# One program per engine for each mixer: attention heads between the last projections, the scan behind the heads

## What is computed

```python
def _mixer(x, w_in, ..., w_out, band_bias, valid):
    u = x @ w_in
    ...
    u_conv, u_lru, q, k, v = jnp.split(u, [o1, o2, o3, o4], axis=-1)
    y_conv = _conv_module(u_conv, ...)
    y_lru = _recurrent(u_lru, ...)
    y_attn = _swa(q, k, v, band_bias, valid, sinks)
    return jnp.concatenate([y_conv, y_lru, y_attn], axis=-1) @ w_out
```

## Time and profile before

| | us |
|---|---|
| three runs | 2514.08, 2515.64, 2520.54 (median 2515.64) |
| profiled execution | 2516.15 |
| its span, first to last instruction | 2514.3 |
| TensorE busy in the span | 2396.6 (95%), 14866 matmuls |
| VectorE busy | 1877.7 (75%) |
| ScalarE busy | 1245.8 (50%) |
| GpSimd busy | 60.3 (2%) |

### The profile page before, as it was taken

How to read it: one execution, slowest core, us unless ns; L and a number is a source line. 1 busy time by engine, 2 the same in 40 slices (tenths; PEclk the granted TensorE clock), 3 DMA queues, 4 the chain that set the end, 5 groups by cost and what they waited for, 6 DMA issues and landing times. The chain is left out here.

```text
span 2514.3 us, 39398 instructions
## 1 busy us (share of the span) xinstructions
PE 2396.6 (95%) x14866; PEld 2130.2 (85%) x14866; DVE 1877.7 (75%) x2802; ACT 1245.8 (50%) x2014; POOL 60.3 (2%) x91
## 2 busy tenths in 40 slices
PE   7998969999989999998999999999999988999998
PEld 3877847888889999886799998899998967999997
DVE  4887578999977776588677776577875796777765
ACT  5345437887734554246345554245552355445541
POOL 0011011000000000000000000000000000000000
PEclk8999979999999999999999999999999999999999
DMA  6774559999943333230223234314334312233332
GB/s 233 278 252 151 197 223 357 412 411 412 347 126 93 104 107 126 87 110 34 68 85 118 85 118 145 87 54 119 91 91 153 93 62 68 68 93 101 110 121 81
DMA packets 312858, 381.50 MB, mean 152 GB/s; under 512 B 16845, under 2 KB 229485, under 8 KB 312567
## 3 DMA queue, kind: packets, MB, share of 16 engines
q1 hardware_dynamic: 303192, 344.59, 40.6%
q0 software_dynamic: 6896, 26.22, 2.8%
q10 hardware_dynamic: 2606, 8.47, 0.8%
HBM read 345.65 MB, written 33.57 MB: 151 GB/s over the span
## 5 line engine op out<-in xcount | busy, mean ns | idle before, releaser
L1740 PE MATMUL PS<-xT_hi,w_part_hi 128*128 128x256 f32 (+1 forms) x1472 | 436.9, 297 | 9.3 <-DVE w_part_lo L1736 3.6
L1742 PE MATMUL PS<-xT_hi,w_part_lo 128*128 128x256 f32 (+1 forms) x1472 | 431.8, 293 | 0.0
L1741 PE MATMUL PS<-xT_lo,w_part_hi 128*128 128x256 f32 (+1 forms) x1472 | 431.5, 293 | 0.0
L2270 DVE TENSOR_TENSOR w_part_lo<-w_raw,w_part_hi 128x512 fp32r<-128x512 f32 x504 | 329.1, 687 | 89.1 <-ACT w_part_hi L2141 88.3
L2141 ACT ACTIVATE w_part_hi<-w_raw 128x512 fp32r<-128x512 f32 x504 | 293.5, 622 | 176.0 <-DVE w_raw L2273 135.5
L1740 PEld LDWEIGHTS PS<-xT_hi,w_part_hi 128*128 128x128 f32 x1472 | 282.7, 192 | 22.9 <-issue 5.3
L1741 PEld LDWEIGHTS PS<-xT_lo,w_part_hi 128*128 128x128 f32 x1472 | 282.9, 192 | 6.8 <-issue 0.4
L1742 PEld LDWEIGHTS PS<-xT_hi,w_part_lo 128*128 128x128 f32 x1472 | 282.6, 192 | 5.4
L1741 PE MATMUL PS<-x_sums,w_part_hi 128*128 128x256 f32 x864 | 244.5, 283 | 0.0
L1742 PE MATMUL PS<-x_sums,w_part_lo 128*128 128x256 f32 x864 | 244.4, 283 | 0.0
L1740 PE MATMUL PS<-x_sums,w_part_hi 128*128 128x256 f32 x864 | 244.3, 283 | 0.0
(11 more groups left out here) (554 smaller groups left out, 5356.2 us busy)
## 6 DMA issues: line engine op xcount, KB each, us to landing
expert_w_raw<-in_w SPq DMA_DIRECT2D x136, 512.0 KB, 7.4
w_raw<-in_ffn_w_gate SPq DMA_DIRECT2D x144, 256.0 KB, 3.1
w_raw<-in_ffn_w_up SPq DMA_DIRECT2D x144, 256.0 KB, 3.4
w_raw<-in_w SPq DMA_DIRECT2D x68, 512.0 KB, 7.5
w_raw<-in_w_in SPq DMA_DIRECT2D x56, 512.0 KB, 4.7
w_raw<-in_ffn_w_down SPq DMA_DIRECT2D x52, 512.0 KB, 4.5
head_rows<-in_ffn_w_down SPq DMA_DIRECT2D x36, 512.0 KB, 5.2
late_raw<-in_w_ada SPq DMA_DIRECT2D x32, 512.0 KB, 5.4
```

Source lines behind the costliest of these rows:

```text
L1740: nc.tensor.matmul(out, a[0][a_at], b[0][b_at], start=first, stop=False, skip_group_check=True)
L1741: nc.tensor.matmul(out, a[0][a_at], b[1][b_at], start=False, stop=False, skip_group_check=True)
L1742: return nc.tensor.matmul(out, a[1][a_at], b[0][b_at], start=False, stop=last, skip_group_check=True)
L2270: V.tensor_tensor(part_lo, part_source(i, step, g), part_hi.bitcast(f32), ALU.subtract).then_inc(z["lo"], 1)
```

## The change

- **One block** for each mixer: the queues of the three programs are joined per engine, and the two waits of all engines within a mixer are gone. SP issues all eight tiles of `w_out` and the next step's first tiles from one list.
- **Order of the projections:** `MIN_ORDER` puts k (12) behind v, then q 8 to 11. Unit 15 is k, units 16 to 19 are the q tiles, two heads each. The first heads' scores follow unit 16; units 17, 18 and 19 stand between the first heads' steps, in banks 7, 6 and 7.
- **Beside the heads:** the three taps on TensorE are made per half of the channels in bank 7 (`last_taps`) in heads 3 and 4, the means in head 6, the variances in head 7; the last nine taps on VectorE (19 to 27) stand between its steps for the heads. The square of the convolved rows moves from VectorE to ScalarE, and so does VectorE's half of the copies of turned probabilities.
- **POOL's product** is released by the gates and not by a block.
- **Behind the heads:** the tanh product, the root's product, the scan and its gate on VectorE (L3186 to L3204), the convolution's norm. Half of the output transposes come before the last head's outputs. `out_rows` takes the attention's four tiles first (`MOUT_ORDER` is now a list of pairs), then the convolution's and the scan's, each with a wait of its own (`conv_ready`).
- The buffers of the probabilities now share their place with the mixer's input tiles and those of `w_out`, closed and opened in turn before the block.

```diff
-    MIN_ORDER = [0, 1, 2, 3, 4, 5, 6, 7, 13, 8, 9, 10, 11, 12]
+    MIN_ORDER = [0, 1, 2, 3, 4, 5, 6, 7, 13, 12, 8, 9, 10, 11]
...
-    MOUT_ORDER = [2, 3, 0, 1]
+    MOUT_ORDER = [(0, 2), (0, 3), (1, 2), (1, 3), (0, 0), (0, 1), (1, 0), (1, 1)]
...
+                    pool.wait_ge(m["gates_out"], 2 * l + 2)
+                    nc.gpsimd.tensor_tensor(xc[:, :, :], xc[:, :, :], i_g[:, :, :], ALU.mult).then_inc(m["gated_in"], 1)
...
+                    def scores(u):
+                        p, at = u % 2, 2 * (u % 2)
+                        if u % 2 == 0:
+                            pe.wait_ge(m["q_lo"], 5 * l + 2 + u // 2)
+                        if u >= 2:
+                            pe.wait_ge(m["scores_read"], U + u - 1)
...
+                    values_turned()
+                    unit(16)
+                    gates(0)
+                    gates(1)
+                    scores(0)
+                    scores(1)
+                    unit(17)
+                    prob_transposes(0)
+                    unit(18)
+                    scores(2)
+                    prob_transposes(1)
+                    unit(19)
+                    outputs(0)
+                    for u in range(2, QH):
+                        if u + 1 < QH:
+                            scores(u + 1)
+                        if u in (3, 4):
+                            last_taps(u - 3)
+                        if u == 6:
+                            means()
+                        prob_transposes(u)
+                        if u == 7:
+                            variances()
+                        outputs(u - 1)
+                        if u == 6:
+                            out_transposes(0)
+                            out_transposes(1)
+                    outputs(QH - 1)
...
+                    for k in range(13, 19):
                         tap(k)
...
+                    qk_lo(12)
+                    tap(19)
+                    qk_lo(8)
+                    tap(20)
+                    maxima(0)
+                    split_lo(T(12))
+                    maxima(1)
+                    tap(21)
+                    tap(22)
+                    row_sums(0)
+                    qk_lo(9)
...
+                    tap(24)
+                    tap(25)
+                    normalised(0)
+                    qk_lo(11)
+                    maxima(3)
```

More of the change, by code:

```diff
@@ L2647, in _ @@
                     norm_rows(sp, s)
+                    for n in range(N_MOUT):
+                        load_tile(sp, Unplaced(TO(0).n + n), mout_src(l, n))
+                    ahead.load(sp)
                 @block.gpsimd
@@ new lines, in means, with variances @@
+                    def means():
+                        pe.wait_ge(m["taps_read"], 3 * l + 3)
+                        for ch in range(2):
+                            last = nc.tensor.matmul(PS[:, 7, :], ones_ch[:, :], conv[:, ch, :], start=ch == 0, stop=ch == 1)
+                        last.then_inc(m["mean_done"], 1)
+                    def variances():
+                        pe.wait_ge(m["sq_done"], l + 1)
+                        for ch in range(2):
+                            last = nc.tensor.matmul(PS[:, 7, :], ones_ch[:, :], sq[:, ch, :], start=ch == 0, stop=ch == 1)
+                        last.then_inc(m["var_done"], 1)
@@ L2678, in _ @@
                     transposes(pe, s, 1)
-                    for u in range(4, 17):
+                    for u in range(4, 16):
                         unit(u)
[L2681 to L2697, removed]
@@ new lines, in _, with out_rows @@
+                    outputs(QH - 1)
+                    def out_rows(n, blocks, start, stop, halves=(0, 1)):
+                        half, kp = MOUT_ORDER[n]
+                        t = TO(n)
+                        for b in blocks:
+                            for kk in halves:
+                                last = product(PS[:, (0 if half else 4) + b, :], XT, (slice(None), 2 * kp + kk, slice(b * P, (b + 1) * P)), (t.hi, t.lo), (slice(None), slice(kk * HALF, (kk + 1) * HALF)),
+                                               n == start and kk == 0, n == stop and kk == 1)
+                        if 1 in halves:
+                            last.then_inc(w_used, 1)
@@ L2705, in _ @@
+                    pe.wait_ge(m["half0_read"], l + 1)
+                    transposes(pe, s + 1, 0)
+                    for n in (2, 3):
+                        out_rows(n, (2, 3), None, 3)
                 @block.scalar
@@ L2779, in _ @@
                     nc.scalar.activation(r_g[:, :, :], sig[:, :, :], ACT.Square).then_inc(m["tanh_out"], 1)
+                    for u in range(3, QH):
+                        softmax(u)
+                        copy_transposed(u - 1)
+                        if u == 5:
+                            split_hi(TO(0))
+                        if u == 6:
+                            split_hi(TO(1))
+                    y_hi(0)
+                    y_hi(1)
+                    act.wait_ge(m["norm_out"], 2 * l + 1)
@@ new lines, in _ @@
+                    y_hi(3)
+                    split_hi(TO(2))
+                    split_hi(TO(3))
+                    act.wait_ge(m["norm_out"], 2 * l + 2)
+                    for ch in range(2):
+                        nc.scalar.activation(sq[:, ch, :], conv[:, ch, :], ACT.Silu, bias=small[:, ch, CNB:CNB + 1], scale=small[:, ch, CG:CG + 1])
+                    act.drain()
+                    nc.scalar.activation(xT_hi[:, 0:2, :], sq[:, :, :], ACT.Copy).then_inc(m["silu_out"], 1)
+                    act.wait_ge(m["o_done"], U + QH)
@@ new lines, in _ @@
+                    tap(10)
+                    tap(11)
+                    split_lo(T(9))
+                    dve.wait_ge(m["evac"], E + 12)
+                    for k in range(LRU_K):
+                        lru_tap(k)
+                    split_lo(T(10))
+                    dve.wait_ge(m["chain_b"], 2 * l + 2)
+                    V.tensor_tensor(lamc[:, :, 4], lamc[:, :, 4], lamc[:, :, 3], ALU.mult)
+                    dve.drain()
+                    V.tensor_tensor(lamc[:, :, 4], lamc[:, :, 4], lamc[:, :, 5], ALU.add)
```

552 lines of the change are left out of this document (269 added, 283 removed).

## The result

| | us | ratio to before, 95% interval |
|---|---|---|
| before, median of four runs | 2517.65 | |
| changed, four runs | 2492.49, 2492.58, 2494.24, 2495.03 (median 2493.41) | 0.9908 [0.9895, 0.9920] |
| its profiled execution | 2495.03, span 2493.2 | |

The change makes the kernel 24 us faster by the medians, 0.9% by the ratio; 2494 was forecast. A whole mixer lies some us earlier or later in one execution than in another: the tile split on ScalarE that stood at 1121.76 before starts at 1122.53 now.

A forecast was written before the change was run, and what follows sets the result against it. VectorE was taken to bound the projections, a chain between engines the attention. 1137.1 + 1.5 + 52.0 + 2.5 + 1.7 + 41.0 = 1235.8 saves 12.5 and 9.9 us, so 2516.15 - 22.4 gives 2494; range 2485 to 2507.

The forecast's parts named there:

- The mark: Turning of the first normalised rows, ending the affected stretch; forecast at 1235.8 against 1248.29 and 1245.67 before.
- step 3: TensorE from first scores to last head's output: list of 52.0 us plus 2.5 of waits at the end.
- Step 1: VectorE's new queue ahead of the first scores: low half of q 8 done at 1137.1, TensorE idling 6 to 8 us.
- Step 2: POOL's product of convolved rows and gate, beside VectorE's queue ahead of the scores: holds up a tap, 1.5 us.
- Step 4: TensorE's clock halved behind the idle stretch ahead of the scores: one such stretch in each mixer, costing 1.7 us.
- Step 5: Output projection up to the turning of the first normalised rows: begins without a seam, 41.0 us including short waits.
- The low end: Fastest whole-run times forecast: near 2485 without penalties and late waits, and 2485 as the range's lower limit.
- the waits of steps 3 and 5: TensorE's waits at the last head, 2.5 us, and in the output projection, about 1.0 plus a last 1.0.
- the bounds of steps 2 to 4: Ends in us: POOL's product 0.23 to 2.37, waits at the last head 0 to 7.0, half clock 0 to 3.4.
- the one without penalties: Rival: POOL's product falls between taps and TensorE's clock holds ahead of the heads; 2487.4 us, chance 0.20.
- That the projections do not cover the heads: Rival: projections between heads delay them as much as they cover; 2512 us, midway 2503, chance 0.13 for 2503 to 2516.
- The clock staying down: Rival: TensorE stays at half clock through the attention; 2520 us at 30 us in each mixer, chance 0.05.

The follow-up runs named there:

- run with POOL's product later: The changed kernel with POOL's product also waiting for the low half of q 8; 2492.10 us, 0.9898 of before.
- run with the copies back: The changed kernel with VectorE again copying one half of each head's turned probabilities; 2493.95 us, 0.9909 of before.
- the two runs without them: Changed kernel with POOL's product waiting for q 8's low half, 2492.10 us; changed kernel with 28 useless products filling TensorE's wait before the first scores, 2489.74 us.

## Why the prediction held

The mark was forecast 12.5 and 9.9 us earlier, 22.4 in all; it came 12.04 and 10.34 earlier, 22.4. That the sums agree so closely is partly luck: single terms are off by up to 1.1 us and cancel, and the scan's part in it is not in the prediction (step 3).

| step | forecast, us | measured, mixer 1 / 2 |
|---|---|---|
| 1: low half of q 8 without POOL, on the clock of before | 1137.1 | 1137.25 (run with POOL's product later: 1136.63 + 1.39, less the 0.77 by which this mixer lies later) |
| 2: POOL's product | 1.5 | 0.68 / 0.66 |
| 3: TensorE's list | 52.0 | 52.7 / 52.7 (first scores to first output row, 57.31 / 56.34, less the two rows below) |
| 3: waits in it | 2.5 | 1.8 |
| 4: clock | 1.7 | 2.8 / 1.8 |
| 5: first output row to mark | 41.0 | 41.10 / 41.10 |

- **Step 1** held: 6.94 us of wait for VectorE ahead of the first scores, 6 to 8 forecast. That the changed queue can be added up from rows of the old one rests on VectorE having no other wait there than the one on ScalarE's split, and that was counted.
- **Step 2** was right in its mechanism and twice too large. I let the next tap begin 0.8 us behind POOL's start; by step 1's own walk the low half of k lies first, to 1134.3, and POOL's product did not hold it (1.39 beside it and without it). So the tap met only the last 0.9 of POOL's 2.35.
- **Step 3** held in what it says of the list, of the three waits at the end (0.3, 0.9, 0.6) and of the copies (run with the copies back). It was incomplete in why: I put the cover down to what stands on TensorE between the heads: the projections first, then the next head's scores, taps or means. The projections do cover the first heads, but putting them first again costs only 2 us of the 24; the scan ahead of head 7's maxima costs 12. In the prediction the scan is a step of the output projection, and that taking it out of the heads frees their chain is said nowhere; the sum was right because TensorE's list at full pace assumes it.
- **Step 4** was too small. One stretch of 3.4 us was taken; it was 6.1 and 3.9 us long, and came behind the wait in both mixers. It is the largest miss of the sum, 1.1 in mixer 1.
- **Step 5** held to 0.1, with one wait of 0.5 in it.
- **The low end** was misreckoned. Without penalties and without the waits of steps 3 and 5 the prediction's own terms give 2480, not 2485, and the bounds of steps 2 to 4 give 2483 as the low end of the range. The forecast does not rest on either.

Of the rivals, the one without penalties (2487) is what the two runs without them point to, if their gains add up: 1.3 less without POOL, 3.7 less without the half clock, 2488. That the projections do not cover the heads fell with the waits: none stands between the first scores and head 7. The clock staying down did not happen.

## What to carry to other kernels

A wait names the engine that came last, not the one that was late: follow it through that engine's queue, as here from TensorE to ScalarE's copies, to the softmax ahead of them, to VectorE's maxima, to a scan that nobody waited for yet. Work that feeds a later stage can cost as long as it stands in the chain of the present one, even where the engine that does it looks idle a quarter of the time; here it was 12 us. When one engine's list has become the bound, look at the wait ahead of its first item: putting four pairs of taps behind the two low halves that TensorE waited for, and POOL's product where VectorE idles, brought 11.7 us more, half of what the whole change brought.

## What the runs showed that I had not expected

- The same wait of 6.9 us was followed by 6.1 us at 1.2 GHz in one mixer and 3.9 in the other, in one execution; the loss of one stretch differs by 1 us between mixers and between kernels that do the same work there. A difference under 1 us a mixer can't be read from marks behind such a wait unless that stretch is measured too and taken out.
- POOL loses time to VectorE as well: 2.86 instead of 2.35 when a tap with both operands in SBUF had begun first.
- Products of no use, put into a wait, made the run 3.7 us shorter.
